# Prompt attention: two heads of each group weighed on VectorE instead of GpSimd

## What is computed

```
def query_block(i):                       # 128 queries; 8 blocks
    s_c = q . ck;  p_c = softmax(s_c, compressed keys that end before the query)
    imp = cmp_to_sel(p_c.sum(heads));  idx = top_k(imp, 16)      # 16 blocks of 64 keys
    s_s = q . k_sel[idx];  p_s = softmax(s_s, causal)
    s_w = q . k_win;       p_w = softmax(s_w, the last 512 keys)
    o = g0 * (p_c @ cv) + g1 * (p_s @ v_sel) + g2 * (p_w @ v_win)
```

## Time and profile before

| | us |
|---|---|
| median of 3 runs | 2328.67 |
| lowest and highest run | 2326.91, 2336.65 |
| the profiled execution | 2326.66 |
| its span (first to last instruction) | 2324.9 |
| PE busy in the span | 1941.5 |
| DVE busy | 1305.1 |
| ACT busy | 1078.6 |
| POOL busy | 225.8 |

### The profile page before, as it was taken

One profiled execution on the slowest core, in us unless ns is written; L12 is line 12 of the kernel. 1 busy time (PEld: TensorE's weight loads), 2 busy tenths in 40 slices (PEclk: granted clock), 3 DMA queues, 4 the chain that ended last, 5 costly groups with the idle time before them and its releaser, 6 DMA issues. The chain is left out here.

```text
span 2324.9 us, 28234 instructions
## 1 busy us (share of the span) xinstructions
PE 1941.5 (84%) x10249; PEld 1536.3 (66%) x10249; DVE 1305.1 (56%) x1954; ACT 1078.6 (46%) x1671; POOL 225.8 (10%) x203
## 2 busy tenths in 40 slices
PE   7899987999978888865976999389999999995640
PEld 2899766999866777720525555278888888874530
DVE  1534324544455677751001366589888889864427
ACT  5311114444266777720110221268887887763324
POOL 0100000000012334300100000001000000000002
PEclk9999997999967999977785899699999999997775
DMA  8411128542145000018581722189999999975517
GB/s 274 114 51 53 65 78 264 225 154 83 40 134 167 19 15 6 5 39 241 142 182 53 270 95 83 51 327 415 426 414 418 413 413 416 409 303 215 222 49 281
DMA packets 155006, 443.06 MB, mean 191 GB/s; under 512 B 37073, under 2 KB 82005, under 8 KB 123209
## 3 DMA queue, kind: packets, MB, share of 16 engines
q1 hardware_dynamic: 135785, 340.78, 39.7%
q0 software_dynamic: 13792, 81.90, 10.4%
q10 hardware_dynamic: 5328, 19.02, 2.0%
HBM read 387.17 MB, written 58.70 MB: 192 GB/s over the span
## 5 line engine op out<-in xcount | busy, mean ns | idle before, releaser
L2719 DVE TENSOR_TENSOR moe_lo<-wts_raw,moe_hi 128x2048 fp32r<-128x2048 f32 x216 | 484.3, 2287 | 59.5 <-ACT moe_hi L2634 59.4
L2634 ACT ACTIVATE moe_hi<-wts_raw 128x2048 fp32r<-128x2048 f32 x216 | 401.2, 1915 | 25.2 <-PE moe_U L2516 25.2
L2502 PE MATMUL moe_G<-moe_hi,moe_xh 128*128 128x512 f32 x288 | 117.8, 409 | 43.2 <-DVE moe_lo L2719 35.5
L872 PE MATMUL cmp_hp<-cmp_xh,cmp_wh 128*128 128x256 f32 (+2 forms) x512 | 151.0, 295 | 0.0
L948 DVE TENSOR_TENSOR cmp_xl<-cmp_bank,cmp_xh 128x512 fp32r<-128x512 f32 (+1 forms) x136 | 82.6, 668 | 121.5 <-ACT cmp_xh L902 121.4
L872 PE MATMUL cmp_hp<-cmp_xh,cmp_wl 128*128 128x256 f32 (+2 forms) x512 | 147.5, 288 | 0.0
L872 PE MATMUL cmp_hp<-cmp_xl,cmp_wh 128*128 128x256 f32 (+2 forms) x512 | 147.4, 288 | 0.0
L1361 POOL TENSOR_SCALAR att_prow<-att_prow,att_scale 128x640 f32<-128x640 f32 (+15 forms) x96 | 113.7, 1197 | 339.4 <-DVE att_scale L1485 339.4
L1458 DVE TENSOR_TENSOR att_pl<-att_pT,att_ph 128x512 fp32r<-128x512 f32 (+5 forms) x148 | 101.3, 688 | 79.5 <-ACT att_ph L1389 79.1
L2542 PE MATMUL moe_Y<-moe_hi,moe_hh 128*128 128x512 f32 x288 | 118.4, 411 | 29.4 <-DVE moe_hl L2735 24.9
L1962 POOL DMA_INDIRECT rou_xg<-s_h,rou_idx x36 | 51.3, 1425 | 882.9 <-PE moe_XT L2521 538.6
(11 more groups left out here) (448 smaller groups left out, 4458.5 us busy)
## 6 DMA issues: line engine op xcount, KB each, us to landing
wts_raw<-in_w_gate SPq DMA_DIRECT2D x72, 1024.0 KB, 7.1
wts_raw<-in_w_up SPq DMA_DIRECT2D x72, 1024.0 KB
wts_raw<-in_w_down SPq DMA_DIRECT2D x72, 1024.0 KB
s_yb<-moe_y ACTq DMA_DIRECT2D x36, 512.0 KB, 7.9
smp_wa<-in_w_ada SPq DMA_DIRECT2D x8, 2048.0 KB
fro_wraw<-in_w_ada SPq DMA_DIRECT2D x4, 2048.0 KB
s_yb<-att_zero SPq DMA_DIRECT2D x1, 8192.0 KB
fro_wraw<-in_w_in SPq DMA_DIRECT2D x12, 512.0 KB
```

The source lines that it names most:

```text
L872: last = pe.matmul(hp[u % 2][:, 0:n], lhs[:, w, :], rhs[:, u % 3, at], start=(r == 0 and t == 0 and m == 0), stop=(r == 1 and t == 7 and m ...
L2502: pe.matmul(G[:, :], xh[k][:, c, :], wh, start=(c == 0), stop=False)
L2634: act.activation(hi[p][half][:, :], raw[p][half][:, :], ACT.Copy).then_inc(hi_ready[p], 1)
L2719: dve.tensor_tensor(lo[p][half][:, :], raw[p][half][:, :], hi[p][half][:, :], ALU.subtract).then_inc(lo_ready[p], 1)
```

## The change

The GpSimd program of the stage is taken out. The vector block's `weigh` gets, behind the product that forms the weights, a wait for that product's own semaphore, `scale_ready`, and then the two products of heads 0 and 1, in place, with the weights as a scalar for each partition. The second one signals `weighed_v`, for which PE waits where it waited for `weighed_p`. ACT's half and the list `order` stay.

```diff
-                    pe.wait_ge(weighed_p, grp + 1)
+                    pe.wait_ge(weighed_v, grp + 1)
                     pe.wait_ge(weighed_a, grp + 1)
...
-        @block.gpsimd
-        def _(pool):
-            for grp, (i, br, g) in enumerate(groups):
-                width = row_keys(i, br)[1]
-                pool.wait_ge(scale_ready, grp + 1)
-                for h in range(QG // 2):
-                    row = prow[br][:, h, 0:width]
-                    last = pool.tensor_scalar(row, row, scale[:, grp, h:h + 1], None, ALU.mult)
-                last.then_inc(weighed_p, 1)
...
                 dve.tensor_tensor(sc, sc, w, ALU.mult).then_inc(scale_ready, 1)
+                dve.wait_ge(scale_ready, grp + 1)
+                for h in range(QG // 2):
+                    row = prow[br][:, h, 0:row_keys(i, br)[1]]
+                    last = dve.tensor_scalar(row, row, scale[:, grp, h:h + 1], None, ALU.mult)
+                last.then_inc(weighed_v, 1)
```

More of the change, by code:

```diff
@@ L1210, in stage_prompt_attention @@
         scale_ready = s.sem("scale_ready")
-        weighed_p = s.sem("weighed_p")
+        weighed_v = s.sem("weighed_v")
         weighed_a = s.sem("weighed_a")
```

## The result

The changed kernel took **2353.84 us** (median of 4 runs, 2351.05 to 2360.40) against 2332.66 us for the kernel before on the same chip: a ratio of 1.0095, with a 95% interval of 1.0058 to 1.0132. A second series (e12) gave 2354.21 against 2334.0 us, 1.0087 [1.0073, 1.0102]. So it is slower by some 20 us, more than the half percent that a measurement can tell from no change. The forecast was 2344 in a range of 2330 to 2355. The sign was right, the time lies at the upper end of the range, and one term was missing from the sum. The kernel before, too, has a higher median here (2332.66 us of 4 runs) than the 2328.67 us of 3 runs that the forecast started from.

The account below looks back on a forecast made before the run. A ring of PE, DVE and ACT bounds the attention stage, no engine being full. 12.1 + 3.0 + 2.0 - 0.4 = 16.7 us on 2326.66 gives 2343.4; the median lying 2.0 us higher, 2344 was written, range 2330 to 2355.

Parts of the forecast that it names:

- The sign: Whole kernel: the change makes it slower, 16.7 us in sum; chance of slower by more than half a percent 0.65.
- behind selected groups: Attention stage, 16 places: products delay the next minimum and so ACT's exponential, less any wait for PE there; 12.1 us.
- behind compressed groups: First groups' 0.4 us delays mostly arrive; second groups' are swallowed in DVE's wait for ACT, blocks 0 to 6; 3.0 us.
- behind window groups: Low part's wait for ACT hides most delay: 1.0 us in block 0, 0.07 at each of 14 others; 2.0 us.
- GpSimd's wait, given back: PE's last wait for GpSimd, at 983.97, and the same place of the block's first group: 0.4 us returned.
- TensorE's clock: Rival: PE's clock falls in longer waits, blocks 4 to 7; 4 to 6 us more, 2348; no separate chance.
- The price of a product: Each further product on DVE costs a slot of 0.132 + N/1920 us, N being the width.
- the delay of a group: From a group's weights to DVE's next instruction, two products and the wait for the weights add 0.38 + N/960 us.
- that rival: GpSimd's wait was the path and DVE's idle time takes the products: 7.7 us come back, 2319; chance 0.10.
- the swallowing one: Rival: delays are swallowed further down by PE's own waits; 8 us stay, 2335; chance 0.20 for 0 to 10 us.

Follow-up runs that it names:

- e12: The changed kernel unchanged, measured and profiled a second time: 2354.21 us against 2334.0 us for the kernel before, ratio 1.0087.
- e3: Against the kernel before, heads 0 and 1 are not weighed by any engine; PE waits for the weights and ACT's half alone: 2330.82 us, ratio 1.0003.
- e5: Against the changed kernel, all 96 products stay on DVE but one unit later, behind the next group's second minimum: 2337.40 us, 1.0009 to the kernel before.
- e1: Against the kernel before, only the selected groups' heads 0 and 1 move to DVE; compressed and window groups stay on GpSimd: 2354.17 us, ratio 1.0093.
- e2: Against the kernel before, only compressed and window groups' heads 0 and 1 move to DVE; selected groups stay on GpSimd: 2339.06 us, ratio 1.0036.
- e4: Against the changed kernel, two more products on a spare tile per selected group, ahead of the real ones: 2371.25 us, 1.0160 to the kernel before.
- e6: Against the kernel before, DVE weighs heads 2 and 3 in ACT's place, one unit later, in all groups; GpSimd keeps 0 and 1: 2336.86 us, ratio 1.0010.
- e9: Against the kernel before, GpSimd also weighs head 2 in window groups, leaving ACT head 3 alone there: 2329.19 us, ratio 0.9972.
- e11: Against the kernel before, GpSimd weighs three of four window rows and all four compressed rows: 2327.00 us, ratio 0.9969.
- e10: Against the kernel before, GpSimd weighs all four rows of the window groups and ACT none there: 2339.42 us, ratio 1.0023.
- e7: Against the kernel before, in window groups alone DVE weighs heads 2 and 3 in ACT's place, one unit later: 2334.80 us, ratio 1.0005.

## Why the prediction was right, and where it was short

The growth of the stage over the second trace of before, by the group behind whose weights it stands, against the prediction's terms:

| term | forecast | after | e12 |
|---|---|---|---|
| behind selected groups, without the clock | 12.1 | 11.3 | 11.3 |
| behind compressed groups | 3.0 | 2.5 | 2.6 |
| behind window groups, without the clock | 2.0 | 0.7 | 0.7 |
| GpSimd's wait, given back | -0.4 | -0.7 | -0.7 |
| TensorE's clock, net | not in the sum | 7.0 | 6.3 |
| sum (rounded) | 16.7 | 20.8 | 20.2 |

The clock's row is the growth of five places and, in after, of a sixth (below), less the delay of the products there, and less 0.3 to 0.5 us that after gains at the first compressed place of block 3. The size of the -0.7 is from e3 and e5, where it stands alone (0.35 us at each of two places); in after and e12 it is part of the selected places of block 7 and is added back in the first row.

**The price of a product and the delay of a group** were right to 0.01 us. They came from four products in a row of another stage, with width and operands alike.

**The selected places** were right one by one: 0.65, 0.65 / 0.78, 0.78 / 0.91, 0.92 in blocks 1 to 3 (forecast 0.64, 0.78, 0.91 each) and 0.61, 0.80 in block 4 (1.42 together). What made that possible is the subtraction of the wait for PE that stood at the same place: this is the whole cover that the products have. Only the two of block 0 came with nothing (0.88 forecast together).

**The compressed places** were right in kind, first groups arriving (0.39 to 0.46), as the second of block 7 did, and the other second ones swallowed; block 4's gave 0.27 for 0.4, and the first one of block 0 nothing.

**The window places** cost 0.4 us in block 0 and about nothing elsewhere; 2.0 us was the bounds' choice and too much.

**GpSimd's wait** was given back at the one place that showed on ACT, and at its twin, 0.35 us each for 0.2. The reading that carried the forecast's sign held: ACT's unbroken row behind the wait meant that the wait was not the path. Neither that rival nor the swallowing one came true.

**The step that failed is the clock.** The prediction had it as a rival of 4 to 6 us with a price from the earlier trace rows, placed it in blocks 4 to 7, and wrote the forecast's 2344 without it. It measured 7.0 us (6.3 in e12), falls behind selected groups of blocks 5 to 7 making 2.0 us of it (1.6) and the window places at the end of block 2 and in block 3 the rest. The right sum was 16.7 less some 2.9 us of small misses, and the clock on top.

That the time lies in the range is in part luck. Of the 9.8 us above 2344, 4.0 come from the higher median of before and 4.5 from the growth (21.2 for 16.7), in which the small misses took back 2.9 of the clock's 7.0 us; the rest is a slip of the prediction, whose own sum, 2343.4 and 2.0, makes 2345.4.

The rows of after, at the end of block 3, and in block 5 its first and second group:

```profile
800.34 0.63 PE L1287 MATMUL att_pT<-one_ident,att_prow 128*128 128x128 f32 x4 [2.38 <-ACT att_prow L1398]
...
803.00 1.12 PE L1341 MATMUL att_op<-one_ident,att_ot 128*128 128x128 f32 x4 [1.32 <-ACT att_ot L1405]
...
870.68 0.50 PE L1311 MATMUL att_S<-att_kT,att_qh 128*128 128x512 f32 x1 [1.06 <-ACT att_prow L1389]
...
896.98 0.62 PE L1311 MATMUL att_S<-att_kT,att_qh 128*128 128x512 f32 x1 [1.06 <-ACT att_prow L1389]
...
898.82 0.82 DVE L1463 TENSOR_REDUCE att_low<-att_S 128x1 f32<-128x640 f32 x1 [2.04 <-PE att_S L1318]
```

The granted clock (PEclk, the last number but two) at the end of block 3 in before and in after, and at the sixth place in after:

```profile
787.10:790.40 3.30, 3.07 (x14) 2.77 (x13) 2.15 (x7) 2.04 (x7) 1.04 (x1) 0.50 0.00 0
...
801.70:811.80 10.10, 8.80 (x32) 7.24 (x32) 5.44 (x14) 5.35 (x17) 0.00 (x0) 0.50 0.00 0
979.20:982.40 3.20, 3.05 (x12) 2.65 (x13) 0.82 (x1) 3.14 (x7) 0.00 (x0) 0.50 0.00 0
```

At 800.34 PE had waited 2.38 us for ACT's half, at 803.00 another 1.32 us, and there four transposes take 1.12 us instead of 0.6: TensorE is at the lower of its two levels (1.2 of 2.4 GHz). It stays there from 801.7 to 811.8, some 10 us, and in before some 3. In block 5 the same wait of 1.06 us ahead of the scores stands in both groups; behind the first a score product takes 0.50 us, behind the second 0.62, and DVE's minimum then waits 2.04 us for the scores instead of 1.36. The sixth place, the first selected one of block 7, has such a fall in after and none in e12, where it is 0.37 us shorter. The falls were there before the change too, as the granted clock of the stage shows (0.89 and 0.88 of full speed before, 0.84 and 0.85 after).

What decides the length of such a stretch stays open. At the end of block 3 the place is 2.3 to 3.7 us longer in after, e1 to e6 and e9 to e11, and not in before (twice) or e7. Even e3 and e5, whose products delay nothing, have 3.4 of after's 5.1 us at the end of block 2 and in block 3, so this part of the term is not the price of the delays alone. Two kernels with the same wait there, before:

```profile
787.04 0.78 PE L1335 MATMUL att_op<-att_ph,att_vv 128*128 128x512 f32 x1
```

and e9, which has no product on DVE:

```profile
783.97 0.63 PE L1296 MATMUL att_pT<-one_ident,att_prow 128*128 128x128 f32 x4 [1.99 <-POOL att_prow L1372]
...
784.35 0.48 PE L1344 MATMUL att_op<-att_ph,att_vv 128*128 128x512 f32 x1
...
792.08 1.11 PE L1296 MATMUL att_pT<-one_ident,att_prow 128*128 128x128 f32 x4
```

Behind the same 1.99 us for GpSimd (the earlier trace rows has before's) PE is slow at once in before (0.78 us for a product of 512); in e9 it goes on at the higher level (0.48), falls some 2 us later, and is still slow at 792.08. So the wait at the place alone does not set the fall. Whether what lay before it in the kernel shifts it, and which part of that, or the execution does, these runs do not tell apart: e1 to e7 and e9 to e11 have one trace each.

## What to carry to other kernels

Idle time of an engine is cover only where the idle time stands in the queue: look up what is behind the new instructions there, subtract the wait that stands at that place, and follow the next result that somebody waits for once around the ring. The same work one unit later in the same queue was free. And before a slow engine is relieved, look whether the receiver of its result ever starts at once behind that wait; a slow engine with nobody queued behind it can be the best place for work, as e9 and e11 show, so long as its result comes in time, which in e10 it did not.

## What had not been expected of the hardware

TensorE's granted clock moved by places, not by stages. The two traces of one kernel agree on most falls, with places equal to 0.2 us, but not on all: block 0 is 2.7 us apart in those of before, one place of block 7 0.37 us in those of after. Another kernel falls elsewhere or for longer (10 us for 3 at the end of block 3), and not only behind an added delay: e3 agrees with the second trace of before to 0.05 us at every place up to the first window group of block 1, and is then 1.1 us shorter behind that, with less time at the lower clock. Products of DVE and GpSimd that run side by side make each other longer. In e7 two of DVE's at 640 took 1.50 us where they took 1.02 alone, with GpSimd's pair unchanged at 3.75 us; in block 7 of e7 DVE's pair took 1.06 us and GpSimd's 4.03; in e6 at 896 both grew (DVE 1.97 us for two of 684 ns, GpSimd 5.39 for 5.02). The sum of both grew by 0.3 to 1 us a pair. (Spans on GpSimd are rough in these profiles.) (The Trainium skill, SBUF — State Buffer, SBUF: two separate sides, has these two engines share a pair of SBUF ports by an exclusive lock, for VectorE instructions in a mode that uses both ports or with two inputs in SBUF, so that the one that comes second stands still for the whole instruction of the other. The traces agree that a lone one pays nothing and that of two one or both pay; they show no stand of a whole instruction, 1.88 us of GpSimd's at 640, and at 968.14 DVE came second and paid 0.04 us.) It was no part of the change, which leaves GpSimd idle.
